# Value weights kept in the rotary tiles, two gate steps ahead of the values, values stored interleaved

## The chip, the cores and the metric

The kernel runs on one core of a Trainium2 chip. The core has a matrix engine (PE, TensorE), a vector engine (DVE), an activation engine (ACT), a general engine (POOL, GpSimd) and a queue engine (SP); each runs its own list of instructions in order, and they meet at semaphores only. Transfers between the main memory and the on-chip memory (SBUF) are issued from SP's or POOL's list and run on 16 DMA engines that all queues share. TensorE runs at one of two clocks, 1.2 or 2.4 GHz; the profile calls the higher one 1.00 and the lower one 0.50.

The metric is the device time of one execution in microseconds (us); lower is better.

## What is computed

The layer is one encoder block on 2048 tokens of 1024 channels. What matters here is its first part, the projections of the normalised input, and who reads them:

```python
h = rmsnorm(x, norm_mix[l])
proj = h @ w_in[l]                                   # 1024 -> 2304
qa, ka, va, qb, kb, vb = jnp.split(proj, splits, axis=-1)
qa = rope(qa.reshape(b, s, A_Q_HEADS, HEAD_DIM), pos)   # 8 heads of 64
ka = rope(ka.reshape(b, s, A_KV_HEADS, HEAD_DIM), pos)  # 2 heads of 64
ya = swa_gqa_sinks(qa, ka, va, attn_sinks[l]) @ w_o_a[l]
yb = chunk_relbias_attention(qb, kb, vb, rel_bias[l]) @ w_o_b[l]   # 8 heads of 64
gates = jax.nn.sigmoid(h @ w_branch_gate[l] + b_branch_gate[l])    # 2 x 1024
```

After it come the gated sum, an output projection, a mixture of 32 experts and a final norm. The change doesn't touch them.

## The kernel before

The kernel is a chain of stages with a barrier of all engines after each: `project`, `attend_b` (branch B), `attend_a` (branch A), then the merge, the routing, the experts and the last sum. Each stage's results go to scratch tensors in main memory and are loaded by the next one.

`project` first normalises and transposes x (0 to 85 us of the trace) into `hT_hi` and `hT_lo`: every number is kept as a high and a low part, and every product is made of three matmuls (high by high, high by low, low by high). Then it runs STEPS = 34 steps, listed by `KINDS`: 6 PLAIN (queries, keys and values of branch A), 8 SPLIT (queries and keys of branch B, stored as two parts), 4 TOKENS (the values of branch B, for four tiles of 128 tokens each) and 16 GATE. A step is 96 matmuls of 128x512 into four of the eight PSUM banks; even steps use banks 0 to 3, odd ones banks 4 to 7 (`eight`).

A PLAIN, SPLIT or GATE step needs one weight tile of 128x1024 (512 KB), and a TOKENS step needs four (`V_CHUNKS`), the same four in each of the four steps. `PIECES` lists the tiles in order of use: 46 pieces. For each piece n SP loads the raw tile into `w_raw[n % 2]` as soon as piece n - 2 is split (`wlo_done`); ACT copies it to `w_hi[n % 2]` (rounding it), once PE is done with piece n - 2 (`mm_done`); DVE writes the rest to `w_lo[n % 2]`; PE waits for `wlo_done`. ACT and DVE work two pieces ahead: their loop over n first splits piece n + 2 and then, if n is the last piece of its step, evacuates the step's four banks (`evacuate`). ACT writes the banks to `f_hi[half]` (a Sigmoid for a gate) and DVE writes the low parts to `f_lo[half]`. SP stores these (`store`), behind the weight load of the same n in its list. PE starts a step only when the banks of the step before the last one are evacuated (`plain_out` or `f_lo_done`).

A TOKENS step is stored by eight DMAs of 256 KB; in the scratch tensor `v_b` of before (head, row, tile, part, 64 channels) each run of 64 channels (256 bytes) lies by itself. `attend_b` loads one head of it by one DMA of 8 KB per row (`load_v`), 1 MB.

Beside this POOL turns the queries and keys of branch A (the rotary part): ROPE_TILES = 5 tiles by four columns are 20 turns. Each issues seven loads into `ro_raw`, `ro_swap`, `ro_cos` and `ro_sin`, waits for them, does five operations, issues four stores (16 turns of queries) or two (4 turns of keys) and waits for those before the next turn. All of these names but `ro_hi` and `ro_lo` are halves of `x_in[0]` to `x_in[2]`, the tiles that held x. After the last turn POOL issues 32 stores of zeros (512 KB each, from `g_row`) into the scratch tensor `ys`.

Of the kernel before, what the change touches and what calls it, by code (L numbers as in the profile page):

```python
# [21 lines left out]
ALU = mybir.AluOpType  # L22
# [94 lines left out]
KINDS = [PLAIN] * A_TILES + [SPLIT] * QK_TILES + [TOKENS] * V_STEPS + [GATE] * GATE_TILES  # L117
STEPS = len(KINDS)
PIECES = [(s, c) for s, kind in enumerate(KINDS) for c in range(V_CHUNKS if kind == TOKENS else 1)]
W_TILES = A_TILES + QK_TILES + V_CHUNKS + GATE_TILES  # L120


def weight_tile(s, c):

    if KINDS[s] == TOKENS:
        return A_TILES + QK_TILES + c
    return s if s < A_TILES + QK_TILES else s - V_STEPS + V_CHUNKS
# [16 lines left out]
def stores_from(s, low):  # L144

    per = {PLAIN: 0 if low else 1, SPLIT: 1, TOKENS: 2, GATE: 0 if low else 1}
    return 16 * sum(per[kind] for kind in KINDS[:s])


def project(nc, x, norm_mix, w_feat, gate_bias, rope_cos, rope_sin, ident, feat, rot_q, rot_k, qk, v_b, gates, blank):  # L150
# [4 lines left out]
    with Stage(nc, "pj") as st:  # L155
# [29 lines left out]
        w_ready = [st.sem(f"w_ready{p}") for p in range(2)]  # L185
        whi_done = st.sem("whi_done")
# [8 lines left out]
        block = st.block()  # L195

        @block.sync
        def _(sp):
# [12 lines left out]
            def store(s, half):  # L211
                cols = slice(half * HALF, (half + 1) * HALF)
                if KINDS[s] in (PLAIN, GATE):

                    sp.wait_ge(plain_out, evacuations(s, (PLAIN, GATE)) - 4 + 2 * half + 2)
                    dst = feat[s] if KINDS[s] == PLAIN else gates[s - STEPS + GATE_TILES]
# [4 lines left out]
                for low, (buffer, stored) in enumerate(((f_hi, hi_stored), (f_lo, lo_stored))):  # L221
                    if KINDS[s] == SPLIT:
                        sp.dma_start(qk[low, s - A_TILES, :, cols], buffer[half][:].bitcast(F32)).then_inc(stored[half], 16)
                    else:
                        for t in range(2):
                            n = (s - A_TILES - QK_TILES) * 4 + half * 2 + t
                            sp.dma_start(v_b[:, :, n, low, :].rearrange("h p d -> p h d"),
                                         buffer[half][:, t * NB:(t + 1) * NB].bitcast(F32).rearrange("p (h d) -> p h d", d=DH)
                                         ).then_inc(stored[half], 16)

            for n, (s, c) in enumerate(PIECES):
                if n + 2 < len(PIECES):
# [11 lines left out]
        def _(pool):  # L244
# [46 lines left out]

            pool.wait_ge(zeros_set, 1)
# [5 lines left out]
        def _(act):  # L298
# [29 lines left out]
            def split_weights(n):  # L328
                act.wait_ge(w_ready[n % 2], n // 2 * 16 + 16)
                if n >= 2:  # L330

                    act.wait_ge(mm_done, n - 1)
                act.activation(w_hi[n % 2][:], w_raw[n % 2][:], ACT.Copy).then_inc(whi_done, 1)  # L333

            def evacuate(s):
                kind = KINDS[s]
                act.wait_ge(mm_done, last_piece(s) + 1)
                for half in range(2):
                    if s > 0:

                        act.wait_ge(hi_stored[half], stores_from(s, False))
                    for b in range(2):
                        bank, cols = eight[s % 2 * 4 + 2 * half + b], slice(b * NB, (b + 1) * NB)
                        if kind == GATE:
                            t = s - STEPS + GATE_TILES
# [17 lines left out]
        def _(dve):  # L363
# [28 lines left out]
            def split_weights(n):  # L392
                dve.wait_ge(whi_done, n + 1)
                dve.tensor_tensor(w_lo[n % 2][:], w_raw[n % 2][:], w_hi[n % 2][:], ALU.subtract).then_inc(wlo_done, 1)  # L394

            def evacuate(s):
                for half in range(2):
# [3 lines left out]
                    for b in range(2):  # L401
                        bank, cols = eight[s % 2 * 4 + 2 * half + b], slice(b * NB, (b + 1) * NB)
                        dve.wait_ge(f_hi_done, evacuations(s, (SPLIT, TOKENS)) - 4 + 2 * half + b + 1)
                        dve.scalar_tensor_tensor(f_lo[half][:, cols], bank[:], scale_of(s), f_hi[half][:, cols],
                                                 ALU.mult, ALU.subtract).then_inc(f_lo_done, 1)
# [10 lines left out]
        def _(pe):  # L416
# [51 lines left out]
            for s in range(head, head + V_STEPS):  # L468
# [1744 lines left out]
```

## Time and profile before

| | us |
|---|---|
| median of 3 runs | 2931.5 |
| lowest and highest of these | 2922.29, 2965.14 |
| the profiled execution | 2918.7 |
| its span, first to last instruction | 2917.1 |
| mean clock of TensorE in it | 0.915 |

| engine | busy us | share of the span |
|---|---|---|
| PE | 2510.5 | 86% |
| PEld (weight loads of PE) | 2071.1 | 71% |
| DVE | 1341.9 | 46% |
| ACT | 1045.2 | 36% |
| POOL | 702.0 | 24% |

PE is busy for most of the span, so what counts is where it is not. The profile cuts the span into 40 slices of 73 us. PE is busy for nine tenths or more from the second slice on, with a dip to 6 and 8 tenths in the sixth and seventh, which is where the four TOKENS steps lie. A timeline names each instruction with its start and length; rows of equal instructions that follow one another are merged (x4). "[5.00 <-X]" behind a row is the time the engine stood idle before it, and what ended that. SPq is SP's queue as it issues DMAs, and "landing" is the time from a DMA's issue until its semaphore is reached.

### The profile page before, as it was taken

To read this page: it belongs to the slowest core of one execution; us is meant where nothing else is said; L and a number is where in the kernel's file an instruction comes from. 1 tells how busy PE (TensorE), PEld (TensorE's weight loads), DVE (VectorE), ACT (ScalarE), POOL (GpSimd) and SP (SyncE) were. 2 spreads that over 40 slices of the span, in tenths; PEclk is the share of its full clock that TensorE was granted. 3 is DMA by queue.
4 is the path that set the end of the run, shared out by engine and by line. 5 is a ranking of instruction groups with operands and counts; after the bars stand their busy time and mean duration, and the time that the engine had idled before them with its cause. 6 is when DMAs were issued, how large, how long until landed. Compare 5 with 4: busy or idle time off the path is not lost. (4 is left out here: it accounts for less than half of the span.)

```text
span 2917.1 us, 37013 instructions
## 1 busy us (share of the span) xinstructions
PE 2510.5 (86%) x12254; PEld 2071.1 (71%) x12255; DVE 1341.9 (46%) x1962; ACT 1045.2 (36%) x1705; POOL 702.0 (24%) x693
## 2 busy tenths in 40 slices
PE   3899986899996999959389999947999999999950
PEld 3788865788884777748288888836888888888840
DVE  7101122100003666626433332256876767787958
ACT  4111111111113566624321111114654646666722
POOL 4264555500000000000022112102332323233342
PEclk9999998999996999959699998968999999999975
DMA  4245566761214544165553433336886868798968
GB/s 138 87 135 168 202 186 182 226 242 65 86 50 125 125 118 97 43 139 127 168 158 126 137 124 113 101 118 246 315 303 230 316 230 316 260 373 316 352 231 330
DMA packets 237631, 540.18 MB, mean 185 GB/s; under 512 B 55840, under 2 KB 90080, under 8 KB 232304
## 3 DMA queue, kind: packets, MB, share of 16 engines
q1 hardware_dynamic: 190160, 400.73, 41.7%
q0 software_dynamic: 27056, 89.67, 9.3%
q10 hardware_dynamic: 20336, 48.77, 4.6%
q8 instruction: 43, 0.70, 0.1%
q14 instruction: 36, 0.29, 0.0%
HBM read 405.07 MB, written 134.02 MB: 185 GB/s over the span
## 5 line engine op out<-in xcount | busy, mean ns | idle before, releaser
L394 DVE TENSOR_TENSOR pj_w_lo<-pj_w_raw,pj_w_hi 128x1024 fp32r<-128x1024 f32 x46 | 61.9, 1350 | 665.0 <-ACT pj_w_hi L333 664.7
L333 ACT ACTIVATE pj_w_hi<-pj_w_raw 128x1024 fp32r<-128x1024 f32 x46 | 48.6, 1059 | 640.2 <-PE pj_bank L436 525.1
L436 PE MATMUL pj_bank<-pj_hT_hi,pj_w_hi 128*128 128x512 f32 x960 | 257.6, 390 | 3.5 <-DVE pj_w_lo L394 3.5
L436 PE MATMUL pj_bank<-pj_hT_lo,pj_w_hi 128*128 128x512 f32 x960 | 257.4, 390 | 0.0
L436 PE MATMUL pj_bank<-pj_hT_hi,pj_w_lo 128*128 128x512 f32 x960 | 257.2, 390 | 0.0
L1767 POOL TENSOR_TENSOR ex_wd_lo<-weights_raw_d,ex_wd_hi 128x1024 fp32r<-128x1024 f32 x64 | 194.5, 3059 | 131.7 <-ACT ex_wd_hi L1792 131.7
L436 PEld LDWEIGHTS pj_bank<-pj_hT_hi,pj_w_hi 128*128 128x128 f32 x960 | 180.7, 188 | 41.3 <-DVE pj_w_lo L394 3.9
L436 PEld LDWEIGHTS pj_bank<-pj_hT_lo,pj_w_hi 128*128 128x128 f32 x960 | 180.8, 188 | 37.6
L436 PEld LDWEIGHTS pj_bank<-pj_hT_hi,pj_w_lo 128*128 128x128 f32 x960 | 180.8, 188 | 37.6
L1414 PE MATMUL mg_y_ps<-mg_aT_hi,mg_w_hi 128*128 128x256 f32 x512 | 156.2, 305 | 56.1 <-DVE mg_aT_lo L1326 49.0
L1857 DVE TENSOR_TENSOR ex_wd_lo<-weights_raw_d,ex_wd_hi 128x1024 fp32r<-128x1024 f32 x64 | 169.2, 2681 | 9.8 <-ACT ex_wd_hi L1792 9.8
L860 POOL MEMSET a_v_raw<- 64x64 f32 x2 | 0.3, 144 | 659.2 <-POOLq L64 659.2
L1922 PE MATMUL ex_g_ps<-ex_wg_hi,ex_xT_hi 128*128 128x512 f32 x360 | 143.2, 398 | 13.8 <-DVE ex_wd_lo L1857 13.8
L1415 PE MATMUL mg_y_ps<-mg_aT_lo,mg_w_hi 128*128 128x256 f32 x512 | 152.0, 297 | 0.0
L1416 PE MATMUL mg_y_ps<-mg_aT_hi,mg_w_lo 128*128 128x256 f32 x512 | 151.6, 296 | 0.0
L1922 PE MATMUL ex_y_ps<-ex_wd_hi,ex_aT_hi 128*128 128x512 f32 x368 | 149.4, 406 | 1.6 <-DVE ex_aT_lo L1863 1.6
L1851 DVE TENSOR_TENSOR ex_wg_lo<-weights_raw_g,ex_wg_hi 128x1024 fp32r<-128x1024 f32 x128 | 147.9, 1215 | 3.6 <-ACT ex_wg_hi L1792 3.6
L1851 DVE TENSOR_TENSOR ex_wu_lo<-weights_raw_u,ex_wu_hi 128x1024 fp32r<-128x1024 f32 x128 | 148.0, 1216 | 2.2
L1414 PEld LDWEIGHTS mg_y_ps<-mg_aT_hi,mg_w_hi 128*128 128x128 f32 x512 | 106.4, 208 | 58.2 <-issue 49.2
L631 DVE CUSTOM_DVE_ANT_0 b_prob<-b_s_ps,b_bias 128x640 f32<-128x640 f32 (+4 forms) x128 | 93.8, 733 | 114.0 <-PE b_s_ps L677 104.4
L1922 PE MATMUL ex_u_ps<-ex_wu_hi,ex_xT_hi 128*128 128x512 f32 x360 | 146.1, 406 | 0.0
L1922 PE MATMUL ex_y_ps<-ex_wd_hi,ex_aT_lo 128*128 128x512 f32 x368 | 145.3, 395 | 0.0
(245 smaller groups left out, 5833.3 us busy)
## 6 DMA issues: line engine op xcount, KB each, us to landing
weights_raw_g<-in_w_exp_gate_dram SPq DMA_DIRECT2D x128, 512.0 KB
weights_raw_u<-in_w_exp_up_dram SPq DMA_DIRECT2D x128, 512.0 KB
weights_raw_d<-in_w_exp_down_dram SPq DMA_DIRECT2D x128, 512.0 KB
scratch_ys<-ex_y ACTq DMA_DIRECT2D x47, 512.0 KB, 4.4
pj_w_raw<-in_w_feat_dram SPq DMA_DIRECT2D x46, 512.0 KB, 5.9
scratch_gates<-pj_f_hi SPq DMA_DIRECT2D x32, 512.0 KB, 3.4
scratch_ys<-pj_g_row POOLq DMA_DIRECT2D x32, 512.0 KB, 16.2
mg_g_in<-scratch_gates SPq DMA_DIRECT2D x128, 128.0 KB, 2.9
```

The lines of the kernel that those rows point to most:

```text
L333: act.activation(w_hi[n % 2][:], w_raw[n % 2][:], ACT.Copy).then_inc(whi_done, 1)
L394: dve.tensor_tensor(w_lo[n % 2][:], w_raw[n % 2][:], w_hi[n % 2][:], ALU.subtract).then_inc(wlo_done, 1)
L436: last = pe.matmul(eight[4 * p + b][:], w[p][:, k * P:(k + 1) * P], h[:, k, b * NB:(b + 1) * NB], start=(k == 0 and n == 0), stop=(k == KD ...
L631: dve.tensor_tensor_reduce(prob[u % 4][:, :m * P], s_ps[:, :m * P], bias[hd % 2][:, (BAND - m) * P:], -1.0, 3e38, ALU.add, ALU.min, neg[:, ...
L860: pool.memset(v_raw[g][:, :CHUNK], 0.0).then_inc(padded, 1)
L1414: pe.matmul(y, w_hi[:, k, cols], aT_hi[:, k, :], start=(k % 4 == 0), stop=False)
L1415: pe.matmul(y, w_hi[:, k, cols], aT_lo[:, k, :], start=False, stop=False)
L1416: last = pe.matmul(y, w_lo[:, k, cols], aT_hi[:, k, :], start=False, stop=(k % 4 == 3))
L1767: pool.tensor_tensor(wd_lo[p][:, j, :], raw.buffer[2][j][:], wd_hi[p][:, j, :], ALU.subtract).then_inc(d_lo_pool, 1)
L1851: dve.tensor_tensor(slabs(lo, m, j), raw.buffer[m][j][:], slabs(hi, m, j), ALU.subtract).then_inc(lo_done, 1)
L1857: dve.tensor_tensor(wd_lo[p][:, j, :], raw.buffer[2][j][:], wd_hi[p][:, j, :], ALU.subtract).then_inc(d_lo_dve, 1)
L1922: last = pe.matmul(out, xT_parts[x][:, k, :], w_parts[w][:, k, cols], start=(k == 0 and c == 0), stop=(k == xT_parts[2] - 1 and c == 2))
```

## The change

Three things change, the first two in `project`:

- The order of the steps is now 6 PLAIN, 8 SPLIT, 2 GATE, 4 TOKENS, 14 GATE.
- The four raw weight tiles of the TOKENS steps are loaded once, into `x_in[0]` to `x_in[3]`, by four DMAs at the end of POOL's rotary loop, ahead of its zeros. Their semaphore is `v_w_in`. ACT and DVE still split them anew for each of the four steps, 16 pieces in all, now from `x_in`. SP loads the 30 other tiles only (`STREAMED`).
- The values are stored in `v_b` of the shape (tile, row, head, part, 64 channels). ACT and DVE write the high and low parts of one tile of tokens interleaved into one buffer, so that a store is 4 KB per row, 512 KB in all, and a TOKENS step has four of them. `attend_b` loads one head in runs of 512 bytes, 16 of them per row.

```diff
-KINDS = [PLAIN] * A_TILES + [SPLIT] * QK_TILES + [TOKENS] * V_STEPS + [GATE] * GATE_TILES
+GATES_FIRST = 2
+KINDS = ([PLAIN] * A_TILES + [SPLIT] * QK_TILES + [GATE] * GATES_FIRST + [TOKENS] * V_STEPS
+         + [GATE] * (GATE_TILES - GATES_FIRST))
...
-    per = {PLAIN: 0 if low else 1, SPLIT: 1, TOKENS: 2, GATE: 0 if low else 1}
+    per = {PLAIN: 0 if low else 1, SPLIT: 1, TOKENS: 1, GATE: 0 if low else 1}
...
+        def raw_of(n):
+
+            s, c = PIECES[n]
+            return x_in[c] if KINDS[s] == TOKENS else w_raw[STREAMED.index(s) % 2]
+
+        def by_head(buffer, low):
+            return buffer[:].rearrange("p (h l d) -> p h l d", l=2, d=DH)[:, :, low, :]
...
-                    if KINDS[s] == SPLIT:
-                        sp.dma_start(qk[low, s - A_TILES, :, cols], buffer[half][:].bitcast(F32)).then_inc(stored[half], 16)
-                    else:
-                        for t in range(2):
-                            n = (s - A_TILES - QK_TILES) * 4 + half * 2 + t
-                            sp.dma_start(v_b[:, :, n, low, :].rearrange("h p d -> p h d"),
-                                         buffer[half][:, t * NB:(t + 1) * NB].bitcast(F32).rearrange("p (h d) -> p h d", d=DH)
-                                         ).then_inc(stored[half], 16)
-
-            for n, (s, c) in enumerate(PIECES):
-                if n + 2 < len(PIECES):
-
-                    sp.wait_ge(wlo_done, n + 1)
-                    sp.dma_start(w_raw[n % 2][:], w_feat[weight_tile(*PIECES[n + 2])]).then_inc(w_ready[n % 2], 16)
-                if n == last_piece(s):
-                    for half in range(2):
-                        store(s, half)
+                    dst = (qk[low, s - A_TILES, :, cols] if KINDS[s] == SPLIT
+                           else v_b[(s - V_FIRST) * 4 + half * 2 + low].rearrange("p h l d -> p (h l d)"))
+                    sp.dma_start(dst, buffer[half][:].bitcast(F32)).then_inc(stored[half], 16)
+
+            for s in range(STEPS):
+                if KINDS[s] != TOKENS and STREAMED.index(s) + 2 < len(STREAMED):
+
+                    j = STREAMED.index(s)
+                    sp.wait_ge(wlo_done, last_piece(s) + 1)
+                    sp.dma_start(w_raw[j % 2][:], w_feat[weight_tile(STREAMED[j + 2])]).then_inc(w_ready[j % 2], 16)
+                for half in range(2):
+                    store(s, half)
...
+            for c in range(V_CHUNKS):
+                pool.dma_start(x_in[c][:], w_feat[A_TILES + QK_TILES + c]).then_inc(v_w_in, 16)
             pool.wait_ge(zeros_set, 1)
...
             def split_weights(n):
-                act.wait_ge(w_ready[n % 2], n // 2 * 16 + 16)
+                s = PIECES[n][0]
+                if KINDS[s] == TOKENS:
+                    act.wait_ge(v_w_in, 16 * V_CHUNKS)
+                else:
+                    j = STREAMED.index(s)
+                    act.wait_ge(w_ready[j % 2], j // 2 * 16 + 16)
                 if n >= 2:
 
                     act.wait_ge(mm_done, n - 1)
-                act.activation(w_hi[n % 2][:], w_raw[n % 2][:], ACT.Copy).then_inc(whi_done, 1)
+                act.activation(w_hi[n % 2][:], raw_of(n)[:], ACT.Copy).then_inc(whi_done, 1)
...
+                    if kind == TOKENS:
+                        act.wait_ge(lo_stored[half], stores_from(s, True))
...
+                        elif kind == TOKENS:
+                            act.activation(by_head((f_hi, f_lo)[b][half], 0), bank[:].rearrange("p (h d) -> p h d", d=DH),
+                                           ACT.Copy).then_inc(f_hi_done, 1)
...
+                        if KINDS[s] == TOKENS:
+                            buffer = (f_hi, f_lo)[b][half]
+                            dve.tensor_tensor(by_head(buffer, 1), bank[:].rearrange("p (h d) -> p h d", d=DH),
+                                              by_head(buffer, 0), ALU.subtract).then_inc(f_lo_done, 1)
...
+            run(head, GATES_FIRST, f_lo_done, evacuations(head - 2, (SPLIT, TOKENS)))
+            for s in range(V_FIRST, V_FIRST + V_STEPS):
+
+                if KINDS[s - 2] == GATE:
+                    pe.wait_ge(plain_out, evacuations(s - 2, (PLAIN, GATE)))
+                else:
+                    pe.wait_ge(f_lo_done, evacuations(s - 2, (SPLIT, TOKENS)))
...
-                sp.dma_start(v_st[hd % 2][:].bitcast(F32), v_b[hd]).then_inc(v_in[hd % 2], 16)
+                sp.dma_start(v_st[hd % 2][:].bitcast(F32), v_b[:, :, hd, :, :].rearrange("n p l d -> p n l d")).then_inc(v_in[hd % 2], 16)
...
-    v_b = scratch("v_b", (HEADS, P, NT, 2, DH))
+    v_b = scratch("v_b", (NT, P, HEADS, 2, DH))
```

ACT's list, before, from the evacuation of the last SPLIT step (banks 5 to 7) to the first rows that evacuate a TOKENS step:

```order
L351 ACTIVATE pj_f_hi0<-pj_bank4 128x512 [waits pj_hi_stored0,pj_mm_done]
L351 ACTIVATE pj_f_hi0<-pj_bank5 128x512
L351 ACTIVATE pj_f_hi1<-pj_bank6 128x512 [waits pj_hi_stored1]
L351 ACTIVATE pj_f_hi1<-pj_bank7 128x512
L333 ACTIVATE pj_w_hi0<-pj_w_raw0 128x1024 [waits pj_mm_done,pj_w_ready0]
L333 ACTIVATE pj_w_hi1<-pj_w_raw1 128x1024 [waits pj_mm_done,pj_w_ready1]
L333 ACTIVATE pj_w_hi0<-pj_w_raw0 128x1024 [waits pj_mm_done,pj_w_ready0]
L333 ACTIVATE pj_w_hi1<-pj_w_raw1 128x1024 [waits pj_mm_done,pj_w_ready1]
L351 ACTIVATE pj_f_hi0<-pj_bank0 128x512 [waits pj_hi_stored0,pj_mm_done]
```

The same place after the change. `pj_x_in0` and `pj_x_in1` are raw weight tiles of the values here, and the rows of L364 evacuate the first and the second of the two gate steps:

```order
L372 ACTIVATE pj_f_hi0<-pj_bank4 128x512 [waits pj_hi_stored0,pj_mm_done]
L372 ACTIVATE pj_f_hi0<-pj_bank5 128x512
L372 ACTIVATE pj_f_hi1<-pj_bank6 128x512 [waits pj_hi_stored1]
L372 ACTIVATE pj_f_hi1<-pj_bank7 128x512
L349 ACTIVATE pj_w_hi0<-pj_x_in0 128x1024 [waits pj_mm_done,pj_v_w_in]
L364 ACT_TABLE_LOAD [waits pj_hi_stored0]
L364 ACTIVATE pj_f_hi0<-pj_bank0,pj_gbias 128x512 [waits pj_mm_done]
L364 ACTIVATE pj_f_hi0<-pj_bank1,pj_gbias 128x512
L364 ACTIVATE pj_f_hi1<-pj_bank2,pj_gbias 128x512 [waits pj_hi_stored1]
L364 ACTIVATE pj_f_hi1<-pj_bank3,pj_gbias 128x512
L349 ACTIVATE pj_w_hi1<-pj_x_in1 128x1024 [waits pj_mm_done,pj_v_w_in]
L364 ACTIVATE pj_f_hi0<-pj_bank4,pj_gbias 128x512 [waits pj_hi_stored0,pj_mm_done]
```

The split of the first value tile, which waits for `pj_v_w_in`, now stands ahead of the evacuation of the first early gate step in ACT's list; before, the splits there waited for `w_raw`, and no evacuation was due until the first TOKENS step had run.

POOL's list before, from the last stores of the last turn of the rotary loop on; L293 and L294 are the loop of the zeros:

```order
L287 DMA scratch_rot_k<-pj_ro_hi 128x512 [waits pj_ro_done]
L287 DMA scratch_rot_k<-pj_ro_lo 128x512
L293 UNCONDITIONAL_BRANCH [waits pj_zeros_set,pj_ro_stored]
L293 ISA
L294 DMA scratch_ys<-pj_g_row 128x1024
L293 REGISTER_ALU
L293 COMPARE_AND_BRANCH
```

The same place after the change:

```order
L296 DMA scratch_rot_k<-pj_ro_hi 128x512 [waits pj_ro_done]
L296 DMA scratch_rot_k<-pj_ro_lo 128x512
L302 DMA pj_x_in0<-in_w_feat_dram 128x1024 [waits pj_ro_stored]
L302 DMA pj_x_in1<-in_w_feat_dram 128x1024
L302 DMA pj_x_in2<-in_w_feat_dram 128x1024
L302 DMA pj_x_in3<-in_w_feat_dram 128x1024
L304 UNCONDITIONAL_BRANCH [waits pj_zeros_set]
L304 ISA
L305 DMA scratch_ys<-pj_g_row 128x1024
L304 REGISTER_ALU
```

The four loads of the values' weights (L302) stand behind the last stores of the turned keys, and wait for these (`pj_ro_stored`). The loop of the zeros follows them; before, it followed the turns at once.

## Rows read from the trace of the kernel before

**Rows 1.** Windows: core time, busy us (instructions) per engine, clock, DMA share, GB/s.
```profile
392.00:532.00 140.00, 96.68 (x386) 78.02 (x385) 31.13 (x32) 24.71 (x32) 76.37 (x92) 0.84 0.67 185
532.00:880.00 348.00, 348.00 (x1537) 288.24 (x1536) 20.78 (x19) 53.98 (x80) 34.53 (x53) 1.00 0.36 128
```

**Rows 2.** Waits, 392 to 532 us: who waited for whom, total, times, longest.
```profile
ACT pj_w_hi L333 <- DMA pj_w_raw<-in_w_feat_dram: 67.5, 8, 21.4
...
PE pj_bank L447 <- DVE pj_w_lo L394: 43.3, 4, 16.0
```

**Rows 3.** Timeline of PE: start, length, what, idle before.
```profile
392.23 1.07 PE L447 MATMUL pj_bank<-pj_w_hi,pj_hT_hi 128*128 128x512 f32 x4
...
447.31 2.07 PE L447 MATMUL pj_bank<-pj_w_hi,pj_hT_hi 128*128 128x512 f32 x4 [15.99 <-DVE pj_w_lo L394]
...
532.08 1.07 PE L436 MATMUL pj_bank<-pj_hT_hi,pj_w_hi 128*128 128x512 f32 x4
...
879.33 1.07 PE L436 MATMUL pj_bank<-pj_hT_hi,pj_w_lo 128*128 128x512 f32 x4
```

**Rows 4.** Timeline of SP's queue during the values.
```profile
428.01 5.90 SPq L227 DMA_DIRECT2D scratch_v_b<-pj_f_hi  x2
...
435.66 14.17 SPq L235 DMA_DIRECT2D pj_w_raw<-in_w_feat_dram  x4
```

**Rows 5.** Timeline of POOL: first loads of pieces 1, 13, 20 and the zeros.
```profile
116.99 0.75 POOL L261 DMA_DIRECT2D pj_x_in<-scratch_feat  x1 [38.12 <-DMA scratch_feat<-pj_f_hi]
...
385.25 0.58 POOL L261 DMA_DIRECT2D pj_x_in<-scratch_feat  x1 [2.95 <-DMA scratch_rot_q<-pj_ro_lo]
...
549.53 0.54 POOL L261 DMA_DIRECT2D pj_x_in<-scratch_feat  x1 [5.51 <-DMA scratch_rot_k<-pj_ro_lo]
...
567.98 0.54 POOL L294 DMA_DIRECT2D scratch_ys<-pj_g_row  x1 [3.33 <-DMA scratch_rot_k<-pj_ro_lo]
```

**Rows 6.** Timeline of POOL: parts of one piece, and single rows of others.
```profile
138.83 0.58 POOL L261 DMA_DIRECT2D pj_x_in<-scratch_feat  x1 [5.01 <-DMA scratch_rot_q<-pj_ro_lo]
...
141.95 0.55 POOL L266 DMA_DIRECT2D pj_x_in<-in_rope_sin_dram  x1
146.07 1.29 POOL L268 TENSOR_TENSOR pj_x_in<-pj_x_in 128x512 f32<-128x512 f32 x1 [3.57 <-DMA pj_x_in<-in_rope_sin_dram]
...
150.72 1.28 POOL L275 TENSOR_TENSOR pj_ro_lo<-pj_x_in,pj_ro_hi 128x512 fp32r<-128x512 f32 x1
...
154.05 1.37 POOL L282 DMA_DIRECT2D scratch_rot_q<-pj_ro_lo  x2
...
220.42 0.58 POOL L261 DMA_DIRECT2D pj_x_in<-scratch_feat  x1 [2.32 <-DMA scratch_rot_q<-pj_ro_lo]
...
408.41 0.59 POOL L261 DMA_DIRECT2D pj_x_in<-scratch_feat  x1 [5.62 <-DMA scratch_rot_q<-pj_ro_lo]
...
422.21 2.15 POOL L275 TENSOR_TENSOR pj_ro_lo<-pj_x_in,pj_ro_hi 128x512 fp32r<-128x512 f32 x1
```

**Rows 7.** Timeline of ACT at the first gate of before.
```profile
554.10 1.06 ACT L333 ACTIVATE pj_w_hi<-pj_w_raw 128x1024 fp32r<-128x1024 f32 x1 [18.76 <-PE pj_bank L436]
555.18 1.28 ACT L346 ACT_TABLE_LOAD   x1
556.47 2.42 ACT L346 ACTIVATE pj_f_hi<-pj_bank,pj_gbias 128x512 f32<-128x512 f32 x4
```

**Rows 8.** Tile pj_w_raw: its loads' time from issue to landing.
```profile
DMA to landing us min/median/max: 3.4/5.9/13.1
```

**Rows 9.** Windows, as rows 1: stores of the values, and the zeros.
```profile
430.00:444.00 14.00, 1.31 (x6) 0.75 (x4) 0.00 (x0) 0.00 (x0) 3.67 (x7) 0.67 1.00 234
568.00:592.00 24.00, 24.00 (x108) 19.88 (x107) 1.23 (x1) 3.37 (x5) 15.37 (x29) 1.00 0.96 351
```

**Rows 10.** Timelines of SP's queue and of PE, first head of branch B.
```profile
891.05 0.43 SPq L556 DMA_DIRECT2D b_v_st<-scratch_v_b  x1
...
918.51 0.56 PE L723 MATMUL b_o_ps<-b_pt_hi,b_v_st 128*128 128x256 f32 x1
```

More of the change, by code:

```diff
@@ L116, with gate_of, weight_tile @@
 PLAIN, SPLIT, TOKENS, GATE = range(4)
-KINDS = [PLAIN] * A_TILES + [SPLIT] * QK_TILES + [TOKENS] * V_STEPS + [GATE] * GATE_TILES
+GATES_FIRST = 2
+KINDS = ([PLAIN] * A_TILES + [SPLIT] * QK_TILES + [GATE] * GATES_FIRST + [TOKENS] * V_STEPS
+         + [GATE] * (GATE_TILES - GATES_FIRST))
 STEPS = len(KINDS)
 PIECES = [(s, c) for s, kind in enumerate(KINDS) for c in range(V_CHUNKS if kind == TOKENS else 1)]
[L120 to L127, printed above, removed]
+V_FIRST = A_TILES + QK_TILES + GATES_FIRST
+STREAMED = [s for s, kind in enumerate(KINDS) if kind != TOKENS]
+def gate_of(s):
+    return KINDS[:s].count(GATE)
+def weight_tile(s):
+    return s if s < A_TILES + QK_TILES else A_TILES + QK_TILES + V_CHUNKS + gate_of(s)
 def last_piece(s):
@@ L185, in project @@
         w_ready = [st.sem(f"w_ready{p}") for p in range(2)]
+        v_w_in = st.sem("v_w_in")
         whi_done = st.sem("whi_done")
@@ L215, in store @@
                     sp.wait_ge(plain_out, evacuations(s, (PLAIN, GATE)) - 4 + 2 * half + 2)
-                    dst = feat[s] if KINDS[s] == PLAIN else gates[s - STEPS + GATE_TILES]
+                    dst = feat[s] if KINDS[s] == PLAIN else gates[gate_of(s)]
                     sp.dma_start(dst[:, cols], f_hi[half][:].bitcast(F32)).then_inc(hi_stored[half], 16)
@@ L344, in evacuate @@
                         if kind == GATE:
-                            t = s - STEPS + GATE_TILES
+                            t = gate_of(s)
                             act.activation(f_hi[half][:, cols].bitcast(F32), bank[:], ACT.Sigmoid,
@@ L393, in split_weights @@
                 dve.wait_ge(whi_done, n + 1)
-                dve.tensor_tensor(w_lo[n % 2][:], w_raw[n % 2][:], w_hi[n % 2][:], ALU.subtract).then_inc(wlo_done, 1)
+                dve.tensor_tensor(w_lo[n % 2][:], raw_of(n)[:], w_hi[n % 2][:], ALU.subtract).then_inc(wlo_done, 1)
             def evacuate(s):
@@ L403, in evacuate @@
                         dve.wait_ge(f_hi_done, evacuations(s, (SPLIT, TOKENS)) - 4 + 2 * half + b + 1)
-                        dve.scalar_tensor_tensor(f_lo[half][:, cols], bank[:], scale_of(s), f_hi[half][:, cols],
-                                                 ALU.mult, ALU.subtract).then_inc(f_lo_done, 1)
+                        if KINDS[s] == TOKENS:
[3 more added lines that the diff above has]
+                        else:
+                            dve.scalar_tensor_tensor(f_lo[half][:, cols], bank[:], scale_of(s), f_hi[half][:, cols],
+                                                     ALU.mult, ALU.subtract).then_inc(f_lo_done, 1)
             split_weights(0)
@@ L467, in _ @@
             run(A_TILES + 2, QK_TILES - 2, f_lo_done, evacuations(A_TILES, (SPLIT, TOKENS)))
-            for s in range(head, head + V_STEPS):
-                pe.wait_ge(f_lo_done, evacuations(s - 2, (SPLIT, TOKENS)))
+            run(head, GATES_FIRST, f_lo_done, evacuations(head - 2, (SPLIT, TOKENS)))
+            for s in range(V_FIRST, V_FIRST + V_STEPS):
+                if KINDS[s - 2] == GATE:
+                    pe.wait_ge(plain_out, evacuations(s - 2, (PLAIN, GATE)))
+                else:
+                    pe.wait_ge(f_lo_done, evacuations(s - 2, (SPLIT, TOKENS)))
                 for c in range(V_CHUNKS):
                     pe.wait_ge(wlo_done, last_piece(s) - V_CHUNKS + 1 + c + 1)
-                    tokens(s % 2, c, (s - head) * 4)
-            run(head + V_STEPS, 2, f_lo_done, evacuations(head + V_STEPS - 2, (SPLIT, TOKENS)))
-            run(head + V_STEPS + 2, GATE_TILES - 2, plain_out, evacuations(head + V_STEPS, (PLAIN, GATE)))
+                    tokens(s % 2, c, (s - V_FIRST) * 4)
+            tail = V_FIRST + V_STEPS
+            run(tail, 2, f_lo_done, evacuations(tail - 2, (SPLIT, TOKENS)))
+            run(tail + 2, STEPS - tail - 2, plain_out, evacuations(tail, (PLAIN, GATE)))
 HEADS = 8
```

## The prediction

> **What bounds the kernel now.** I read the engines' shares first: PE is busy for 86% of the span, so a change pays or costs where PE stands still. The slices show one dip inside `project`, and the windows of that stage give its size [rows 1]: in the 140.0 us from 392 to 532 PE is busy for 96.68 us, and before and behind it (532 to 880) all the time. The reader should see that PE alone sets the pace there, with DVE and ACT busy for 31 and 25 us of the 140, and that 0.84 in the clock column means that part of the stretch ran at the lower of the two clocks.
>
> The timeline of PE gives the size of a step [rows 3]. Sixteen gate steps run from 532.08 to 879.33 + 1.07 = 880.40 us, which is 348.3 or **21.77 us a step** without a gap. The four TOKENS steps run from 392.23 to 532.08, 139.9 us where 4 x 21.77 = 87.1 would do. So **52.8 us** are lost there. The list of waits says to whom [rows 2]: 43.3 us in four waits for `w_lo`, which waited for ACT, which waited 67.5 us for DMAs of `w_raw`. The other 9.5 us, 2.4 for each stop, are the restarts: after the 15.99 us of one wait four matmuls take 2.07 us and not 1.07 [rows 3], the lower clock.
>
> SP's queue shows why the weights are late [rows 4]: two stores of the values in small runs hold it for 5.90 us, and the four next weight loads for 14.17, while the DMA engines are busy for the whole of 430 to 444 us and move 234 GB/s [rows 9]. Those 52.8 us are what the change can win.
>
> The last view is POOL's timeline, since the change hangs the weights onto its list. The first of the 20 turns starts at 116.99 us, the 13th at 385.25, the zeros behind the 20th at 567.98 [rows 5]. That is 22.4 us a turn at first and 182.7 / 8 = 22.8 for the last eight. **The rotary loop ends 176 us after the values begin.**
>
> **The change, part by part.** *Gates first.* PE reaches the end of the SPLIT steps at 392.2 as before, since nothing ahead of it changes. Two gate steps bring it to 392.2 + 2 x 21.77 = **435.7 us**. Their weight tiles are split two pieces ahead, and their banks are free, as the SPLIT steps were evacuated. Then it stops: the next weights come from POOL.
>
> *When POOL is done.* Its turns are made of parts [rows 6]: issuing seven loads 141.95 + 0.55 - 138.83 = 3.67 us, waiting for them 3.57, arithmetic 146.07 to 152.00 = 5.93, a gap and the issue of the stores to 155.42 = 3.42, and a wait for their landing of 2.32 (at 220.42) to 5.62 (at 408.41). The shortest parts sum to 18.9 us; a turn of the keys, with two stores, took 567.98 - 549.53 = 18.45 [rows 5]. Once the values' stretch begins the DMA engines now have hardly anything else: the last stores of a SPLIT step and one weight load. ACT waits for `v_w_in` ahead of the first gate's evacuation, so nothing else is evacuated or stored. So I take near the shortest. The 13th turn, which had issued its last store at 408.41 - 5.62 = 402.8 and waited 5.62 behind four weight loads, now waits about 3.5: it ends at 406.3. Three more query turns at 19.2 make 463.9, four key turns at 18.4 make **537.5 us**. By the shortest parts throughout it would be 535.6, at the pace of before 568.0.
>
> *The four loads.* POOL needs 0.54 us to issue a DMA of that size [rows 5], 2.2 for four. A `w_raw` load of the same size lands in 3.4 to 13.1 us, 5.9 in the median [rows 8]; four with nothing ahead of them should lie between the first two, so 5.6 to 8.1 us from the first issue. I take 7: weights there at 544.5.
>
> *Behind them on ACT.* The step behind the gates uses the banks of the first gate, and ACT holds that evacuation behind the split. The rows of the first gate of before give the price [rows 7]: split 1.06, table load 1.28, four Sigmoids 2.42, with gaps 4.79 us from start to end. DVE's part of the split runs beside the evacuation. PE starts the values at **549.4 us**, after 113.7 us of standing still. The second gate's evacuation waits for the first gate's stores, but has a whole step of time.
>
> *From there on.* One restart at 2.4 us, then 4 + 14 steps at 21.77 = 391.9: PE ends `project` at 549.4 + 2.4 + 391.9 = **943.7 us** instead of 880.4.
>
> *Stores of the values.* Four of 512 KB instead of eight of 256 KB a step, without the small runs. The stops that they caused are already in the 52.8. ACT and DVE write the same number of elements in the same number of instructions, in strided runs; even 20% more on 2.4 us would hide behind a step of 21.77. ACT's new wait for `lo_stored` has a whole step of cover too.
>
> *The zeros.* 16.8 MB at 351 GB/s are 48 us [rows 9]. They ran beside gate steps with PE busy for 24.00 of 24 us, and run now beside the first two value steps, which load no weights and store 2 MB each. If a store came late by more than a step's slack PE would wait; I price that at 0, at most 10 us.
>
> *Loading the values in branch B.* A head's load is 1 MB in runs of 512 bytes, which no row has. The 256-byte runs went at 234 GB/s [rows 9], so it takes at most 4.5 us, against 3.0 at 351. The first is issued at 891.05 and used at 918.51 [rows 10], 27 us later, behind loads that don't change; the others are issued a whole head ahead. Price 0, at most 3 us in all.
>
> One rule speaks against POOL as the issuer. A row shows what it is about: the subtraction at 422.21 took 2.15 us, its like at 150.72 took 1.28 [rows 6], while DVE was at work. The Trainium skill, "SBUF — State Buffer", section "SBUF: two separate sides", says that POOL and DVE share a pair of SBUF ports under an exclusive lock, and that a DMA issued from POOL can stand waiting for its descriptors while DVE works. By that rule turns and loads would be slower only beside a busy DVE; during this stop DVE waits for the same weights, so by the rule too the arithmetic takes its 5.93 us and the sum stays; with DVE busy in every turn it would be some 0.9 us a turn more, 70 us instead of 63.
>
> **The sum.** 113.7 + 2.4 us of new standstill less the 52.8 of before: **+63.3 us**. On the profiled execution that is 2918.7 + 63.3 = 2982.0. The three runs lie at 2922.3 to 2965.1, their median 12.8 us above the profiled one; on the median it would be 2994.8. I take 2988, between the two.
>
> **The rivals.**
>
> *The loop keeps its pace.* If the 22.8 us a turn are POOL's own and not the crowding of the DMA engines, the loop ends at 568.0 and the cost is 30.5 more, 94 us: 3013 to 3025. For it: from 117 to 385, with less traffic, a turn took 22.4 as well. Against it: the parts that swell are the waits for landing (2.32 against 5.62), and the 20th turn took 18.45.
>
> *Within 2%.* The bound is about 58.5 us. The shortest parts everywhere give 60.0; it takes waits for landing shorter by a further 0.2 us in each of the seven turns, or the scatter of the runs, which is several us on a median.
>
> *Faster.* The same edits win if the weights come in time. PE would have no stop: 435.7 + 391.9 = 827.6, 52.8 less than before, 2866 to 2879. What decides is the end of the rotary loop. The two kernels break even when PE starts the values at 880.4 - 391.9 - 2.4 = 486.1, so with a loop that ends at 474. That leaves 68 us for seven turns, 9.7 each, and the issue and the arithmetic alone take 13.0 of a query turn. Only if the loads didn't wait for the turns could this be, and POOL's list says that they do.
>
> *More than one stop.* Values in 512-byte runs late for branch B, or stores late beside the zeros: +3 to +13 on top, 2991 to 3008.
>
> **How the numbers follow.** Chances: forecast (+59 to +75) 0.60, loop at its old pace 0.10, more than one stop 0.05, within 2% 0.22, faster 0.03. About 2% is what a measurement of this kernel can tell from no change. Slower by over 2% are the first three, 0.75; within 0.22; faster 0.03. The range for eight in ten: from 2970, the shortest parts and low runs with some us of scatter, to 3024, the old pace of the loop on the median of before.
>
> **What would show it.** In the profile of the changed kernel PE should have one wait of about 114 us before the first matmul of L473, ending near 549, and none of the four waits of before. POOL's first load of L302 should start at 535 to 540, with the seven turns before it at about 19 us; PE's last matmul of the stage should end near 944; and what follows should be as long as before. A start of L302 near 568 would prove the old pace, one before 500 would refute the forecast. A wait of PE between 549 and 944 would be the last rival's.

## The result

| | before | changed |
|---|---|---|
| median, us | 2926.89 | 2981.36 |
| lowest and highest, us | 2920.29, 2965.14 | 2978.53, 2992.56 |
| runs | 4 | 4 |
| the profiled execution, us | 2918.7 | 2978.89 |

The changed kernel takes 1.022 times as long (95% interval 1.0192 to 1.0248). Ratios leave out executions that are over 1.5% above the fastest of their kernel, like that of 2965.14 us, and medians don't, so a ratio isn't the quotient of two medians. The predicted time was 2988.0 with a range of 2970 to 3024; it was right in direction, and the measured 2981.4 is 6.6 us from it. The bound of 2% lies inside the interval: that the kernel got slower is clear, that it did so by over 2% is not.

### The profile page after: what moved, and what is told of

It is laid out like the page before. It is cut to its first block and busy times, and to the rows that moved or that the text cites. A ratio compares the mean times of both kernels' runs of the same rounds, so it can differ in the third digit from the quotient of the medians.

```text
span 2977.3 us, 36987 instructions
## 1 busy us (share of the span) xinstructions
PE 2497.3 (84%) x12254; PEld 2061.7 (69%) x12255; DVE 1337.8 (45%) x1962; ACT 1045.1 (35%) x1705; POOL 694.3 (23%) x697
## 5 line engine op out<-in xcount | busy, mean ns | idle before, releaser
L415 DVE TENSOR_TENSOR pj_w_lo<-pj_w_raw,pj_w_hi 128x1024 fp32r<-128x1024 f32 x30 | 38.7, 1294 | 525.1 <-ACT pj_w_hi L349 525.0
L349 ACT ACTIVATE pj_w_hi<-pj_w_raw 128x1024 fp32r<-128x1024 f32 x30 | 31.7, 1060 | 498.0 <-PE pj_bank L462 489.2
L1953 PE MATMUL ex_y_ps<-ex_wd_lo,ex_aT_hi 128*128 128x512 f32 x368 | 145.2, 395 | 0.0
## 6 DMA issues: line engine op xcount, KB each, us to landing
scratch_ys<-pj_g_row POOLq DMA_DIRECT2D x32, 512.0 KB, 21.8
```

What stands on the lines that cost most here:

```text
L349: act.activation(w_hi[n % 2][:], raw_of(n)[:], ACT.Copy).then_inc(whi_done, 1)
L415: dve.tensor_tensor(w_lo[n % 2][:], raw_of(n)[:], w_hi[n % 2][:], ALU.subtract).then_inc(wlo_done, 1)
L1953: last = pe.matmul(out, xT_parts[x][:, k, :], w_parts[w][:, k, cols], start=(k == 0 and c == 0), stop=(k == xT_parts[2] - 1 and c == 2))
```

## The profile after

PE's waits in the first 1000 us, where the four of [rows 2] stood before:

```profile
PE pj_bank L473 <- ACT pj_f_hi L364: 114.3, 1, 114.3
...
PE pj_bank L462 <- DVE pj_w_lo L415: 3.5, 1, 3.5
...
PE pj_bank L473 <- DVE pj_w_lo L415: 0.9, 1, 0.9
```

One wait of 114.3 us has taken the place of four with 43.3 together; the 3.5 us is the start of the steps, as before. The windows show where it lies (columns as in [rows 1]):

```profile
392.00:436.00 44.00, 42.33 (x187) 34.72 (x185) 3.99 (x5) 1.92 (x4) 27.50 (x35) 1.00 0.41 132
436.00:549.00 113.00, 0.34 (x1) 0.34 (x2) 1.23 (x1) 5.15 (x7) 68.97 (x98) 0.52 0.36 115
549.00:640.00 91.00, 90.07 (x390) 74.04 (x390) 26.79 (x28) 25.73 (x34) 9.25 (x18) 0.98 0.64 256
640.00:944.00 304.00, 303.52 (x1340) 250.98 (x1338) 18.32 (x17) 45.27 (x70) 0.00 (x0) 1.00 0.20 73
```

Through the two early gates PE is busy but for the last 1.7 us, then it works for 0.34 us in 113, the DMA engines are busy for about a third of the time (0.36), and behind that it is busy again but for 1.4 us in all. POOL is the engine that works meanwhile. Its timeline, first loads of the 13th, 14th and 17th turn, the values' weights and the first zeros; these answer to [rows 5]:

```profile
384.13 0.59 POOL L270 DMA_DIRECT2D pj_x_in<-scratch_feat  x1 [4.37 <-DMA scratch_rot_q<-pj_ro_lo]
...
406.50 0.58 POOL L270 DMA_DIRECT2D pj_x_in<-scratch_feat  x1 [4.92 <-DMA scratch_rot_q<-pj_ro_lo]
...
463.47 0.58 POOL L270 DMA_DIRECT2D pj_x_in<-scratch_feat  x1 [2.33 <-DMA scratch_rot_q<-pj_ro_lo]
...
534.77 2.10 POOL L302 DMA_DIRECT2D pj_x_in<-in_w_feat_dram  x4 [2.77 <-DMA scratch_rot_k<-pj_ro_lo]
536.88 0.54 POOL L305 DMA_DIRECT2D scratch_ys<-pj_g_row  x1
```

And ACT from the arrival of the weights on, which answers to [rows 7]:

```profile
543.82 1.06 ACT L349 ACTIVATE pj_w_hi<-pj_x_in 128x1024 fp32r<-128x1024 f32 x1 [149.90 <-DMA pj_x_in<-in_w_feat_dram]
544.89 1.28 ACT L364 ACT_TABLE_LOAD   x1
546.19 2.42 ACT L364 ACTIVATE pj_f_hi<-pj_bank,pj_gbias 128x512 f32<-128x512 f32 x4
548.48 1.07 ACT L349 ACTIVATE pj_w_hi<-pj_x_in 128x1024 fp32r<-128x1024 f32 x1
555.32 1.26 ACT L364 ACTIVATE pj_f_hi<-pj_bank,pj_gbias 128x512 f32<-128x512 f32 x2 [5.77 <-DMA scratch_gates<-pj_f_hi]
558.88 1.27 ACT L364 ACTIVATE pj_f_hi<-pj_bank,pj_gbias 128x512 f32<-128x512 f32 x2 [2.30 <-DMA scratch_gates<-pj_f_hi]
```

ACT stood still for 149.90 us, until DMA brought the weights; then came the split, the table load and the four Sigmoids, and PE:

```profile
548.66 2.07 PE L473 MATMUL pj_bank<-pj_w_hi,pj_hT_hi 128*128 128x512 f32 x4 [114.33 <-ACT pj_f_hi L364]
...
554.06 1.07 PE L473 MATMUL pj_bank<-pj_w_lo,pj_hT_hi 128*128 128x512 f32 x4
...
562.41 1.19 PE L473 MATMUL pj_bank<-pj_w_hi,pj_hT_hi 128*128 128x512 f32 x4 [0.93 <-DVE pj_w_lo L415]
...
942.45 1.07 PE L462 MATMUL pj_bank<-pj_hT_hi,pj_w_lo 128*128 128x512 f32 x4
```

PE ends the steps of `project` at 942.45 + 1.07 = 943.5 us instead of 880.4 [rows 3], 63.1 us later. The total grew by 60.2 us only (spans 2977.3 and 2917.1). The other 2.9 us can't be read as a gain of the change: how far the changed kernel lay behind was 63.3 us at the first scores of branch B, 58.4 at its last products, 59.8 at the end of the merge. In branch B TensorE was granted a clock of 0.91 in place of 0.90, with the same instructions:

```profile
965.00:1305.00 340.00, 325.27 (x1678) 238.53 (x1679) 208.58 (x447) 204.89 (x447) 0.00 (x0) 0.91 0.42 97
```

```profile
902.00:1247.00 345.00, 330.56 (x1681) 242.57 (x1681) 208.84 (x447) 204.89 (x447) 0.00 (x0) 0.90 0.38 95
```

The first fence is the changed kernel, the second the kernel before. Both hold low-clock stretches at different moments, and the kernels below scatter in this stage by more.

PE stands still in later stages too: its slices of the kernel before fall to 3 tenths at the lowest there, and to 8, 6 and 8 in the sixth to eighth, which hold the values. Only these three are the change's.

## The experiments

Each ratio is to the kernel before, run on the same chip in the same job. The medians of before differ a little between the jobs (2927.07 beside the first four kernels, 2919.23 beside the next four), so ratios are what is compared. The changed kernel itself was not run again in these jobs: where a total or a moment of it stands beside one of theirs, it is that of its profiled execution above. `gates4`, `gates0`, `zeros_late` and `sp_loads` ran once each.

### Weights in tiles of their own: `own2`

```diff
+        v_raw = [st.sb(f"v_raw{p}", [P, D]) for p in range(3)] + [x_in[3]]
...
-        ro_hi, ro_lo = st.sb("ro_hi", [P, NB], F32R), st.sb("ro_lo", [P, NB], F32R)
+        ro_hi, ro_lo = x_in[2][:, NB:2 * NB].bitcast(F32R), st.sb("ro_lo", [P, NB], F32R)
...
-            return x_in[c] if KINDS[s] == TOKENS else w_raw[STREAMED.index(s) % 2]
+            return v_raw[c] if KINDS[s] == TOKENS else w_raw[STREAMED.index(s) % 2]
...
+            sp.wait_ge(tr_done, NT)
+            for c in range(V_CHUNKS):
+                sp.dma_start(v_raw[c][:], w_feat[A_TILES + QK_TILES + c]).then_inc(v_w_in, 16)
...
-            for c in range(V_CHUNKS):
-                pool.dma_start(x_in[c][:], w_feat[A_TILES + QK_TILES + c]).then_inc(v_w_in, 16)
```

> The changed kernel with its order of steps (two gates ahead) and its stores, but the values' weights lie in tiles that the rotary loop doesn't use (three new ones and x_in[3]), and SP loads them at about 83 us; the space comes from putting ro_hi into the unused half of x_in[2]. Theory 'behind the loop': the loss is only that the four loads wait for the last turn. Then PE has no stop between the gates and the values, all 52.8 us of before are gone too, and the time is 2918.7 - 52.8 = 2866, ratio to before 0.982. Rival 'the new order costs by itself' (first gates between the SPLIT and TOKENS steps, table load and evacuation in ACT's way, interleaved buffers, 512-byte loads in branch B): stops stay at the values or appear in branch B, and the time stays above 2880.

Measured: 2861.73 us, ratio 0.9792 (0.9742 to 0.9841). The stretch of [rows 1], in this kernel:

```profile
392.00:532.00 140.00, 140.00 (x619) 115.95 (x618) 37.64 (x39) 34.98 (x48) 82.81 (x99) 1.00 0.50 167
```

PE is busy for 140.00 of 140 us, at the high clock throughout. Only the place, the time and the queue of four loads were changed (and, for space, the place of `ro_hi`), and the whole cost turned into the gain that the once-loaded weights can give. What the queue is worth by itself is looked at in `sp_loads`. The rival, a cost of the new order itself, is out.

### More gates ahead of the values: `gates8`, `gates4`, `gates0`

```diff
-GATES_FIRST = 2
+GATES_FIRST = 8
...
-            run(head, GATES_FIRST, f_lo_done, evacuations(head - 2, (SPLIT, TOKENS)))
+            run(head, 2, f_lo_done, evacuations(head - 2, (SPLIT, TOKENS)))
+            run(head + 2, GATES_FIRST - 2, plain_out, evacuations(head, (PLAIN, GATE)))
```

The second and third have 4 and 0 in the first line; with 0 the `run` of the gates is left out.

> The changed kernel with eight gate steps ahead of the values instead of two; loads still behind the rotary loop. The values are reached at 392.2 + 8 x 21.77 = 566.4 us. Theory 'behind the loop': the loop, with gate stores beside it again, ends at 540 to 558, weights 7 to 9 later, so PE hardly stops: below 5 us of wait, total 2866 to 2872. Rival 'POOL's loads are slow or the loop stretches with the gates' traffic': the loop ends at 568 or later as in the kernel before, PE waits 12 us and more, 2880 and above.

> Four gate steps ahead instead of two. Theory 'behind the loop': the moment at which the weights come hardly moves (537 to 546 for the first load), and two more steps lie ahead of it, so PE's one stop shrinks from 114.3 us to 70 to 80 and the time falls by 35 to 43.5 us, to about 2940. Rival 'the order costs by itself': no fall in step with the number of gates.

> No gate step ahead of the values, else as changed: weights loaded once behind the rotary loop. Theory 'behind the loop': PE stops at 392 until about 547, a stop of some 155 us instead of 114.3, and the time rises by 41 us to about 3019. This is what the loads alone would have cost without the gates as cover. Rival 'the order costs by itself': the time falls when the gates go back.

| gates ahead | loop ends, us | PE's stop, us | its second stop, us | last matmul of the 34 steps starts, us | profiled execution, us |
|---|---|---|---|---|---|
| 0 | 530.1 | 152.2 | 4.5 | 988.7 | 3025.66 |
| 2 (changed kernel) | 534.8 | 114.3 | 0.9 | 943.1 | 2978.89 |
| 4 | 539.9 | 72.8 | 0.5 | 903.6 | 2949.15 |
| 8 | 550.9 | none | 0.7 | 828.1 | 2863.68 |

The table is the clearest picture of the cause. PE's list up to the stop grows by 43.5 us with each pair of gates, and the stop shrinks by 38 to 42 us, since the weights come 5 us later with each pair: the loop's turns are slower while SP stores a step and loads a weight tile beside them. The 14th turn took 19.1 us in the changed kernel, with no step stored beside it, and 21.9 in `gates4`. The lists of waits of `gates0` and `gates4`:

```profile
PE pj_bank L473 <- DVE pj_f_lo L430: 152.2, 1, 152.2
...
PE pj_bank L473 <- DVE pj_w_lo L415: 4.5, 1, 4.5
...
PE pj_bank L473 <- ACT pj_f_hi L364: 72.8, 1, 72.8
```

The second stop comes after half of the first value step, in all four kernels: ACT must wait for stores before it can go on to the third weight tile. In `gates0` these are the stores of the last SPLIT step but one, which the missing weights had held up, and ACT waited 7.66 and 4.61 us for them. That second stop, with a restart of its own, is why `gates0` ends its steps 45.6 us later than the changed kernel although its long stop is only 37.9 us longer.

With 8 gates the weights come just in time. ACT waited for them, but PE did not stop ahead of the values:

```profile
560.58 1.06 ACT L349 ACTIVATE pj_w_hi<-pj_x_in 128x1024 fp32r<-128x1024 f32 x1 [34.22 <-DMA pj_x_in<-in_w_feat_dram]
```

PE reached the values at 566.2, and its one stop was the 0.7 us of the table. The median of `gates8` is 2862.87 us, ratio 0.9779 (0.9728 to 0.9831), which can't be told from that of `own2`. So the changed kernel's own idea works once eight gates stand ahead and not two. Five to seven were not run; with seven PE would have reached the values about 21.8 us sooner, at 544.4, far ahead of weights that came at 560.58 with eight. The totals of `gates4` and `gates0` are single executions: at the end of the steps they differ from the changed kernel by -39.5 and +45.6 us, in the total by -29.7 and +46.8. I had expected `gates4` to fall by 35 to 43.5; the step did, and the later stages took back 10 us in that one execution.

### The weights alone and the stores alone: `own_only`, `layout_only`

The first is the kernel before with the own tiles of `own2` and nothing else of the change (no early gates, the stores and `v_b` of before). The second is the kernel before with the interleaved stores, the new `v_b` and the head loads in 512-byte runs, and nothing else. From the edit of the second:

```diff
-                    if KINDS[s] == SPLIT:
-                        sp.dma_start(qk[low, s - A_TILES, :, cols], buffer[half][:].bitcast(F32)).then_inc(stored[half], 16)
-                    else:
...
+                    dst = (qk[low, s - A_TILES, :, cols] if KINDS[s] == SPLIT
+                           else v_b[(s - A_TILES - QK_TILES) * 4 + half * 2 + low].rearrange("p h l d -> p (h l d)"))
+                    sp.dma_start(dst, buffer[half][:].bitcast(F32)).then_inc(stored[half], 16)
```

> The kernel before with the values' weights loaded once by SP at about 83 us into tiles that the rotary loop doesn't use; order of steps and the small-run stores as before. Theory 'only the late weights stop PE': with nothing to load in the values' stretch the small-run stores hold nobody that PE waits for, no stop is left, ratio 0.982 (2866 on the scale of 2918.7). Rival 'the stores cost PE too' (ACT and DVE wait for f_hi and f_lo to be stored, and PE for their evacuation): stops of several us remain, ratio 0.985 to 0.995.

> The kernel before with one part of the change only: values interleaved by ACT and DVE, stored in four 512 KB stores a step, v_b of the new shape, head loads in 512-byte runs. Weights are streamed 16 times and the order of steps is as before. Question: how much of the 52.8 us lost at the values was the stores' holding SP and the DMA engines, and how much the streaming itself. Theory 'stores hold up the weights': the first stop (4.6 us behind stores that are not in small runs) is what streaming costs by itself, 7 us with the restart; the other three shrink to it, 28 us of 52.8 are left, time about 2894 to 2900 on the scale of 2918.7 (ratio 0.991). Rival 'streaming alone': stops stay near 43 us, ratio 1.0.

`own_only` measured 2861.35 us, ratio 0.981 (0.9745 to 0.9875). In the values' stretch of that kernel, with the small-run stores in place:

```profile
392.00:480.00 88.00, 88.00 (x390) 72.86 (x389) 33.16 (x33) 25.72 (x35) 52.27 (x64) 1.00 0.69 166
```

PE has no gap, here or in the whole of 392 to 532 us. The DMA engines are as busy as before (0.69, where [rows 1] has 0.67), and PE waits for nobody. With no weights to load beside them the small-run stores cost nothing.

`layout_only` measured 2901.3 us, ratio 0.9939 (0.9921 to 0.9957). Its stretch, its waits, and the longest of its four stops:

```profile
392.00:532.00 140.00, 113.85 (x461) 92.28 (x460) 35.02 (x37) 27.74 (x37) 76.17 (x92) 0.90 0.63 203
```

```profile
PE pj_bank L455 <- DVE pj_w_lo L397: 26.2, 4, 9.0
```

```profile
442.36 2.08 PE L455 MATMUL pj_bank<-pj_w_hi,pj_hT_hi 128*128 128x512 f32 x4 [8.98 <-DVE pj_w_lo L397]
```

The stops fell from 43.3 to 26.2 us, not to the 18 or so that I had expected: each is 5.1 to 9.0 us, and the first of them, behind stores that aren't in small runs, is 5.49. The steps end 17.2 us sooner (last matmul at 862.8 for 880.0), where I had said 25. So storing without the small runs takes away a third of the 52.8 us while the weights are streamed, and the other two thirds stay with the streaming. The two shares belong to this order of removal: `own_only` takes away the streaming alone, and with it all of the 52.8.

### No gates ahead, own tiles: `own0`

> As own2 (own tiles, new stores), but with no gate step ahead of the values. Tells whether the two early gates are worth anything once the weights don't wait for the loop. By the theory nothing: same time as own2, 2866 on the scale of 2918.7, no wait of PE in the values. Rival: the gates ahead give the stores or the evacuations room, and this one is slower by some us.

This is `own2` with `GATES_FIRST = 0`. Measured: 2858.44 us, ratio 0.9789 (0.971 to 0.9868). PE's last matmul of the steps starts at 826.1 us, at 825.8 in `own2` and 825.9 in `own_only`. With the weights in time, neither the order nor the store layout is worth anything that these runs can tell.

### Who issues the loads, and the zeros behind them: `sp_loads`, `zeros_late`

```diff
+                if s == A_TILES + QK_TILES:
+                    sp.wait_ge(ro_stored, (ROPE_TILES - 1) * (SEQ // NB) * 64 + (SEQ // NB) * 32)
+                    for c in range(V_CHUNKS):
+                        sp.dma_start(x_in[c][:], w_feat[A_TILES + QK_TILES + c]).then_inc(v_w_in, 16)
```

This is SP's list in `sp_loads`, and the same loads are gone from POOL's. In `zeros_late` POOL keeps them, and one line stands ahead of the zeros:

```diff
+            pool.wait_ge(mm_done, last_piece(V_FIRST + V_STEPS - 1) + 1)
             pool.wait_ge(zeros_set, 1)
```

> The changed kernel, but SP issues the four loads of the values' weights, into the same tiles x_in, after waiting for the last store of the rotary loop; POOL goes on to the zeros at once. In the changed kernel 9.1 us pass from POOL's first load (534.8) to ACT's first split (543.8). Theory 'behind the loop': the wait is for the turns, the issuing queue is a matter of some us; PE's stop stays at 114 us, give or take 3, and the total near 2979. Rival 'POOL as the issuer costs' (the shared port, software-made descriptors): the weights come 3 us and more sooner behind the loop's end, and the stop falls below 111 us. With the zeros now ahead of them or beside them on another queue they can also come later; then the crowding by the zeros, not the issuer, sets the last part.

> The changed kernel, but POOL waits for the last value step before it issues the zeros. The changed kernel has a second, small stop of 0.9 us after the first quarter of the first value step: ACT waited 5.8 and 2.3 us for the first gate's stores before it evacuated the second gate, and split the third value tile late. Theory 'the zeros crowd out these stores': the waits on the stores shrink to under 3 us in all and the 0.9 us stop goes; the total falls by about 1 us, inside the scatter. Rival 'ACT's order alone': the stop stays.

In `sp_loads` SP issued the loads at 534.86 us, and ACT could start later than in the changed kernel:

```profile
545.62 1.06 ACT L351 ACTIVATE pj_w_hi<-pj_x_in 128x1024 fp32r<-128x1024 f32 x1 [151.12 <-DMA pj_x_in<-in_w_feat_dram]
```

| | first load issued | ACT's first split | between |
|---|---|---|---|
| changed kernel (POOL, zeros behind) | 534.77 | 543.82 | 9.1 |
| `sp_loads` (SP, zeros on POOL beside) | 534.86 | 545.62 | 10.8 |
| `zeros_late` (POOL, no zeros) | 536.61 | 544.38 | 7.8 |

PE's stop was 115.5 us in `sp_loads` and the total 2978.91, as good as the changed kernel's. Letting SP issue the loads gains nothing here, which is enough against the rival that POOL as the issuer makes the stop. The rest is finer than single executions can settle: with the zeros behind them on POOL's queue, the time from the first load to ACT's split is 8.7 to 9.7 us in the changed kernel, `gates0`, `gates4` and `gates8`, so the zeros cost 1 to 2 us there; in the 3.0 us between `sp_loads` and `zeros_late` the zeros beside the loads and the other issuer are mixed. Without them ACT's waits for the first gate's stores shrank from 5.77 and 2.30 us to 0.68 and 0.65:

```profile
550.79 1.26 ACT L365 ACTIVATE pj_f_hi<-pj_bank,pj_gbias 128x512 f32<-128x512 f32 x2 [0.68 <-DMA scratch_gates<-pj_f_hi]
552.71 1.27 ACT L365 ACTIVATE pj_f_hi<-pj_bank,pj_gbias 128x512 f32<-128x512 f32 x2 [0.65 <-DMA scratch_gates<-pj_f_hi]
```

PE's second stop of 0.9 us was gone, and the last matmul of the steps started at 942.2 instead of 943.1. That is the 1 us that I had expected. The total of this single execution is 2968.11, 10.8 us less, of which the steps hold 0.9. Branch B holds another 8.4 (331.3 us instead of 339.7); `own0`, with its zeros early, shows the same 331.3, so I take it for scatter; one execution can't show that.

## Why the prediction was right

Point by point, in its own order:

- **Gates first.** PE should stop at 435.7; its last group there starts at 433.26, so it stopped at 434.3. The stage had begun 1.1 us sooner (first matmul at 84.0 for 85.1; the other kernels here lie between 83.9 and 85.4). Right.
- **The loop's end.** 537.5 was forecast and 534.77 measured, just ahead of the 535 to 540 that the prediction asked for. The 13th turn ended at 406.50 (406.3). The three query turns took 19.0 us each (19.2). The four key turns took 71.3 us (73.6): three of them 17.3 to 17.5 us, shorter than the one row that I had, and one 19.1. The choice between "near the shortest parts" and "the old pace" was the main judgement of the sum, and it held: with the DMA engines quiet (busy share 0.28 from 436 to 534 us) the waits for landing of the stores were 2.29 to 2.77 us. The rival of the old pace is refuted by `gates8` too, where gates are stored beside the loop and it still ended at 550.9 and not at 568.
- **The four loads.** 7 us forecast, 9.1 measured, outside my 5.6 to 8.1. This is the one term of the sum that fell outside its own bounds. I left out the zeros, whose first stands in POOL's list right behind the fourth load; `zeros_late` gives 7.8 without them.
- **Behind them on ACT.** 4.79 us forecast to the start of PE; from 543.82 to 548.66 it was 4.84. PE should start at 549.4 and did at 548.66: the loop was 2.7 us early, the loads 2.1 late. That the two errors cancel is luck.
- **The restart.** 2.4 us forecast. Four groups of four matmuls took 554.06 - 548.66 = 5.40 us where 3.63 would do, so 1.8. The 2.4 itself was a remainder: read in the same way, the four restarts of before cost 1.6, 2.3, 2.7 and 2.3 us.
- **The zeros and the second gate.** I priced the crowding of the stores at 0, at most 10. ACT waited 5.77 and 2.30 us for the first gate's stores, and that reached PE once, as the idle time ahead of 562.41, where the group starts 1.09 us later than in the rhythm of the others. By the prediction's own sign, a wait of PE between 549 and 944 us, this is the rival "more than one stop", at 1 us where it had 3 to 13 and by the gate's stores, not the values'. In `zeros_late` it is gone.
- **The end.** 943.7 forecast, 943.5 measured. The delay at that point, 63.1 us, is the 63.3 of the sum. The closeness is better than the terms: the restart was 0.6 us shorter, and the second stop 1.1 us that had no term.
- **Branch B.** Price 0, and the wait ahead of its first scores is 21.9 us, 21.8 before. The first values were used at 981.80, 63.3 us later than before like all around it. But the load took longer than I had said, see below.
- **DVE beside the turns.** DVE did nothing from 436 to 534 us, as the sum had it, and the five operations of the 16th turn took 5.83 us (451.89 to 457.72), for its 5.93. The 70 us for a DVE that is busy in every turn did not come.
- **The total.** 60.2 us in the profiled executions and 54.5 between the medians, where the execution of 2965.14 us lifts that of before. The sum was right for its stage; the stages behind it scatter by several us with the clock. On the profiled execution the sum gave 2982.0, which is 0.6 us from the median; the likeliest time, set 6 us above that because the median of the three executions of before stood 12.8 us above the profiled one, was 6.6 us too high.
- **The other side.** The rival "faster" asked for a loop that ends by 474 us or for loads that don't wait for the turns. `own2` is the second of these; `gates8`, where the values are reached later, is a way that I hadn't named. They gave 0.979 and 0.978 where 2866 / 2918.7 = 0.982 was worked out.
- **The share of the small-run stores.** The prediction said that these stops "are already in the 52.8", which is right, and named the two stores and the weight loads of [rows 4] together. Their shares came only from `layout_only`: 17 us and 36.

## What to carry to other kernels

A tile that is reused gets its new load only when its last reader is done, and the queue and the moment of that load are set by the slowest user of the tile, not by who needs the data. Before reusing a tile, look up when its present user ends (here 568 us) against when the new data are wanted (392 us); work moved ahead as cover must fill that whole distance, and here two steps of 21.8 us were put where eight were enough. The other way is a tile of its own, loaded early. Here it took one idle tile and three new ones, with 2 KB per row of their space from an unused half tile. It gave the same time as eight gates ahead (0.979 and 0.978), and it doesn't hang on when the loop ends.

## What the runs showed of the hardware that was not expected

The first load in 512-byte runs held the queue that issued it. The next DMA in SP's list behind the values' load of the first head before, and then the load and the next DMA after the change:

```profile
891.53 0.45 SPq L546 DMA_DIRECT2D b_k_st<-scratch_qk  x1
...
954.18 0.44 SPq L587 DMA_DIRECT2D b_v_st<-scratch_v_b  x1
954.65 10.62 SPq L577 DMA_DIRECT2D b_k_st<-scratch_qk  x1
```

The issue of the values' load itself took 0.44 us, that of the next load 10.62, where it took 0.45 before. In `layout_only` it took 10.58, so the change of the layout brings it. Behind the later loads of the values the next DMA came 4.3 us or more after the load, and where its row stands by itself its issue took about 0.5 us. That the hold didn't matter was luck of the order: the first head's queries and keys were already issued. I had priced the load itself at 4.5 us at most, from a rate of other transfers; the eight of them landed after 5.8 to 17.1 us, beside the other loads of the stage:

```profile
DMA to landing us min/median/max: 5.8/7.2/17.1
```

The restart of TensorE didn't cost more after a longer stop. After 152.2 us in `gates0` the first groups took 2.08, 1.91, 1.91 and 1.46 us instead of 1.07, about 3.0 us lost, at the low clock (0.50 from 543.79 to 549.08). But after stops of about 115 us it cost 1.6 us in `zeros_late`, 1.8 in the changed kernel and 2.8 in `sp_loads`, and after stops of 5 to 16 us, in the kernel before and in `layout_only`, anything from 1.5 to 3.0. So many short stops lose more by restarts than one long one.

```profile
543.79 2.08 PE L473 MATMUL pj_bank<-pj_w_hi,pj_hT_hi 128*128 128x512 f32 x4 [152.20 <-DVE pj_f_lo L430]
545.66 1.91 PE L473 MATMUL pj_bank<-pj_w_lo,pj_hT_hi 128*128 128x512 f32 x4
547.37 1.91 PE L473 MATMUL pj_bank<-pj_w_hi,pj_hT_lo 128*128 128x512 f32 x4
549.08 1.46 PE L473 MATMUL pj_bank<-pj_w_hi,pj_hT_hi 128*128 128x512 f32 x4
```

What stays open is the scatter behind the steps: the same instructions of branch B took 344.6 us in the kernel before, 339.7 in the changed one and 331.3 in `own0`, at mean clocks of 0.90, 0.91 and 0.94. No run here was made to find what sets them.
